# Stick-breaking attention on one Trainium2 core: the sum over later keys carried as one row instead of as a tile

## The reference

```python
z = jnp.einsum('bthd,bshd->bhts', q, k) * (SB_HEAD_DIM ** -0.5)
mask = k_pos[None, :] < q_pos[:, None]
log_fail = jnp.where(mask, jax.nn.log_sigmoid(-z), 0.0)
after = lax.cumsum(log_fail, axis=3, reverse=True) - log_fail
a = jnp.where(mask, jnp.exp(jax.nn.log_sigmoid(z) + after), 0.0)
return jnp.einsum('bhts,bshd->bthd', a, v)
```

## Time and profile before

| what | value |
|---|---|
| median of 3 runs | 1157.36 us |
| the profiled execution | 1159.81 us |
| its span, first to last instruction | 1158.0 us |
| TensorE busy | 1109.8 us, 96% |
| VectorE busy | 739.9 us, 64% |
| ScalarE busy | 466.6 us, 40% |
| GpSimd busy | 278.6 us, 24% |
| chain that ended last | TensorE 88%, VectorE 6%, ScalarE 2% |

### The profile page before, as it was taken

One profiled execution on the slowest core, in us unless ns is written; L12 is line 12 of the kernel. 1 busy time (PEld: TensorE's weight loads), 2 busy tenths in 40 slices (PEclk: granted clock), 3 DMA queues, 4 the chain that ended last, 5 costly groups with the idle time before them and its releaser, 6 DMA issues.

```text
span 1158.0 us, 17212 instructions
## 1 busy us (share of the span) xinstructions
PE 1109.8 (96%) x6486; PEld 1039.7 (90%) x6486; DVE 739.9 (64%) x1347; ACT 466.6 (40%) x923; POOL 278.6 (24%) x306
## 2 busy tenths in 40 slices
PE   3999999999999999999999999999999999999994
PEld 2899988999988999988999987999999999999993
DVE  7747986787986787986787995764332312352228
ACT  4345544155544155543146545346022232242221
POOL 2113422213422213422114422110211100121225
PEclk9999999999999999999999999999999999999997
DMA  6023021115021115021115021205111111111144
GB/s 241 19 71 117 19 91 55 39 46 164 19 92 55 40 39 171 20 91 55 39 40 171 19 91 55 101 19 179 56 37 37 54 39 37 43 49 37 38 182 163
DMA packets 41458, 84.89 MB, mean 73 GB/s; under 512 B 2080, under 2 KB 22176, under 8 KB 41248
## 3 DMA queue, kind: packets, MB, share of 16 engines
q1 hardware_dynamic: 40800, 81.43, 21.6%
q10 hardware_dynamic: 576, 2.36, 0.6%
HBM read 67.27 MB, written 16.52 MB: 72 GB/s over the span
## 4 chain that ended last, share of the span: by engine, by line
PE 88%; DVE 6%; ACT 2%; DMA 1%; issue 1%; SPq 0%; DVEq 0%; ACTq 0%
PE bank L623 56%; PE bank L909 9%; PE bank L699 5%; PE bank L739 5%; PE bank L832 2%; PE bank L855 2%; PE bank L686 2%; PE bank L685 2%; DVE xw L1344 1%; DVE imaskL L1303 1%; DVE yb L1614 1%; PE bank L873 1%; PE bank L783 1%; PE bank L761 1%; DVE St L1530 1%
## 5 line engine op out<-in xcount | busy, mean ns | idle before, releaser
L623 PE MATMUL bank<-xl,wh 128*128 128x384 f32 x1344 | 459.0, 342 | 6.7 <-DVE xl L1340 6.7
L623 PE MATMUL bank<-xh,wh 128*128 128x384 f32 x1344 | 454.9, 338 | 4.3 <-ACT xh L1090 3.5
L623 PE MATMUL bank<-xh,wl 128*128 128x384 f32 x1344 | 456.7, 340 | 0.0
L623 PEld LDWEIGHTS bank<-xl,wh 128*128 128x128 f32 x1344 | 253.5, 189 | 14.3 <-DVE xl L1340 8.1
L623 PEld LDWEIGHTS bank<-xh,wh 128*128 128x128 f32 x1344 | 253.8, 189 | 13.5 <-issue 10.6
L623 PEld LDWEIGHTS bank<-xh,wl 128*128 128x128 f32 x1344 | 253.9, 189 | 7.9 <-issue 4.2
L1244 DVE CAST wh<-wr 128x1024 fp32r<-128x1024 f32 x64 | 51.1, 798 | 102.3 <-PE bank L623 102.3
L1034 ACT ACTIVATE slot<-bank,ngate 128x384 f32<-128x384 f32 x48 | 27.7, 578 | 190.7 <-PE bank L623 188.0
L1701 POOL TENSOR_TENSOR imaskH<-i_nat,k 128x512 fp32r<-128x512 f32 (+1 forms) x36 | 50.5, 1407 | 188.1 <-PE bank L832 188.1
L1246 DVE TENSOR_TENSOR wl<-wr,wh 128x1024 fp32r<-128x1024 f32 x64 | 93.1, 1454 | 2.2
L1713 POOL TENSOR_TENSOR slot<-slot,slot 128x384 f32<-128x384 f32 x24 | 32.7, 1364 | 241.0 <-DVE slot L1579 240.8
(11 more groups left out here) (193 smaller groups left out, 1749.1 us busy)
## 6 DMA issues: line engine op xcount, KB each, us to landing
wr<-wch SPq DMA_DIRECT2D x64, 512.0 KB, 3.7
KTc<-ckT SPq DMA_DIRECT2D x4, 2048.0 KB, 8.9
Vc<-cv SPq DMA_DIRECT2D x4, 2048.0 KB, 8.3
xw<-xT SPq DMA_DIRECT2D x6, 768.0 KB, 10.1
graw<-gated SPq DMA_DIRECT2D x8, 576.0 KB, 5.8
xres<-xT SPq DMA_DIRECT2D x1, 4608.0 KB, 16.6
yT<-yb SPq DMA_DIRECT2D x6, 576.0 KB, 3.0
okT<-kT ACTq DMA_DIRECT2D x4, 576.0 KB, 3.0
```

Source lines behind the costliest of these rows:

```text
L623: i = nc.tensor.matmul(CH[n % 2][:, 0:WIN], weights[:, k, :], rows[:, k, w * WIN:(w + 1) * WIN], start=(m == 0), stop=(m == 23))
```

## The change

The sum over later keys is the same for every key of a tile, and it is already in the bank of the tile before: the log-weight of that tile's first key is its score less the softplus of all its keys and of all later ones. So the kernel after keeps one row. ScalarE copies row 0 of the raw scores to `zr[n % 3]` between Exp and Ln. When the subtraction and the last Exp of that step are done, `later_row` on VectorE subtracts the copy from row 0 of the bank and splits the difference into row 0 (high) and row 32 (low) of `RT[h]`, whose other rows are zero. TensorE adds both with one matmul by `rows_r`, a matrix with ones in rows 0 and 32. `SUM`, `SUH` and `SUL` and all their instructions are gone. Since the bank is now read by `later_row`, the scores of step n also wait for its first instruction for step n - 3. Apart from this the last third of the finish moves from GpSimd to VectorE.

```diff
@@ tensor
                         need(pe, s_a, t - 2)
+                        if n >= 3:
+                            need(pe, s_S, SUMS * p + sums_until(n - 3))
-                        c0 = min(c0, QW // 2)
+                        c0 = row_col(n)
...
                         else:
                             pe.wait_ge(s_sph, SPLITS * p + rows_until(m))
                             add(negtri_r[:, :], SPH[m % 2], c0)
-                            cs = first_col(m - 2)
-                            if q == 1:
-                                pe.wait_ge(s_S, SUMS * p + sums_until(m - 2))
-                                add(negones, SUM[h], cs)
-                            else:
-                                pe.wait_ge(s_Sh, SUM_SPLITS * p + sum_rows_until(m))
-                                add(negones_r[:, :], SUH[h], cs)
-                                pe.wait_ge(s_Sl, SUM_SPLITS * p + sum_rows_until(m))
-                                add(negones_r[:, :], SUL[h], cs)
+                            pe.wait_ge(s_Sl, SUMS * p + sums_until(m - 2))
+                            add(rows_r[:, :], RT[h], row_col(m - 2))
@@ scalar
-                        need(act, s_S, SUMS * p + (sums_until(n - 3) if n >= 3 else 0))
                         nc.scalar.activation(E[n % 3][:, c0:QW], Z[n % 3][:, c0:QW], ACT.Exp).then_inc(s_E, 1)
+                        if STEPS[n][1] > 0:
+                            need(act, s_Sl, SUMS * p + (sums_until(n - 3) if n >= 3 else 0))
+                            nc.scalar.activation(zr[n % 3][0:1, row_col(n):QW], Z[n % 3][0:1, row_col(n):QW], ACT.Copy)
@@ vector
+            def later_row(p, m):
+                h, cols = STEPS[m][2], slice(row_col(m), QW)
+                row = zr[m % 3][0:1, cols]
+                dve.wait_ge(s_a, NS * p + m + 1)
+                V.tensor_tensor(row, Z[m % 3][0:1, cols], row, ALU.subtract).then_inc(s_S, 1)
+                dve.wait_ge(s_S, SUMS * p + sums_until(m))
+                dve.wait_ge(s_rz, 2 * (p + 1))
+                V.tensor_copy(RT[h][0:1, cols], row).then_inc(s_Sh, 1)
+                dve.wait_ge(s_Sh, SUMS * p + sums_until(m))
+                V.tensor_tensor(RT[h][32:33, cols], row, RT[h][0:1, cols].bitcast(F32), ALU.subtract).then_inc(s_Sl, 1)
...
-                        if q > 1:
-                            cs = first_col(n - 2)
-                            dve.wait_ge(s_S, SUMS * p + sums_until(n - 2))
-                            V.tensor_copy(SUH[h][:, cs:QW], SUM[h][:, cs:QW]).then_inc(s_Sh, 1)
-                            dve.wait_ge(s_Sh, SUM_SPLITS * p + sum_rows_until(n))
-                            V.tensor_tensor(SUL[h][:, cs:QW], SUM[h][:, cs:QW], SUH[h][:, cs:QW].bitcast(F32),
-                                            ALU.subtract).then_inc(s_Sl, 1)
+                    if 2 <= n <= NS + 1 and STEPS[n - 2][1] > 0:
+                        later_row(p, n - 2)
...
-                for lo, hi in ((0, 3), (3, 6)):
+                for i, (lo, hi) in enumerate(Y_ROWS):
@@ gpsimd
-                    if 1 <= n <= NS and tile_rank(n - 1) == 1:
-                        later_sum(n - 1)
-                    if n < NS and STEPS[n][1] > 0 and tile_rank(n) != 1:
-                        later_sum(n)
...
-            def finish(w):
-                y, x = yb[:, 6:8, w * WIN:(w + 1) * WIN], xres[:, 6:8, w * WIN:(w + 1) * WIN]
...
```

More of the change, by code:

```diff
@@ L180, in rows_until, with row_col @@
     return sum(tile_rank(i) > 0 for i in range(n + 1))
-def sum_rows_until(n):
-    return sum(tile_rank(i) > 1 for i in range(n + 1))
-SPLITS, SUM_SPLITS = rows_until(NS - 1), sum_rows_until(NS - 1)
+SPLITS = rows_until(NS - 1)
+def row_col(n):
+    return min(first_col(n), QW // 2)
 SW = PAST + P
@@ L271, in build @@
         negtri_r, _ = take("negtri_r", [P, P], F32R)
-        negones_r, _ = take("negones_r", [P, P], F32R)
+        rows_r, _ = take("rows_r", [P, P], F32R)
         bm, _ = take("bm", [P, NBLK + STREAMS])
@@ L281, in build @@
         SPL = [take(f"SPL{i}", [P, QW], F32R)[0] for i in range(2)]
-        SUM = [take(f"SUM{h}", [P, QW])[0] for h in range(2)]
-        SUH = [take(f"SUH{h}", [P, QW], F32R)[0] for h in range(2)]
-        SUL = [take(f"SUL{h}", [P, QW], F32R)[0] for h in range(2)]
+        RT = [take(f"RT{h}", [P, QW], F32R)[0] for h in range(2)]
+        zr = [take(f"zr{i}", [P, QW])[0] for i in range(3)]
+        off[0] += 4 * QW
         aw_o = off[0]
@@ L382, in build @@
         s_sp = sem("softplus")
-        s_S = sem("later_sum")
+        s_S = sem("later_row")
+        s_rz = sem("later_rows_zeroed")
         s_sph = sem("softplus_high")
         s_spl = sem("softplus_low")
-        s_Sh = sem("later_sum_high")
-        s_Sl = sem("later_sum_low")
+        s_Sh = sem("later_row_high")
+        s_Sl = sem("later_row_low")
         s_cr = sem("masks_rounded")
@@ L491, in attention_over @@
             need(eng, s_a, NS * (p + 1))
-            need(eng, s_S, SUMS * (p + 1))
+            need(eng, s_Sl, SUMS * (p + 1))
         def recurrence_over(eng, p, norm=True):
@@ L586, in _ @@
             for w in range(NW):
-                for lo, hi in ((0, 3), (3, 6), (6, 8)):
-                    if lo < 6:
-                        sp.wait_ge(s_yo, 2 * w + lo // 3 + 1)
-                    else:
-                        sp.wait_ge(s_yo3, w + 1)
+                for i, (lo, hi) in enumerate(Y_ROWS):
+                    sp.wait_ge(s_yo, 3 * w + i + 1)
                     r = slice(lo, hi)
@@ L1332, in _ @@
             V.tensor_copy(negtri_r[:, :], negtri).then_inc(s_cr, 1)
-            V.tensor_copy(negones_r[:, :], negones).then_inc(s_cr, 1)
+            V.memset(rows_r[:, :].bitcast(F32), 0.0).then_inc(s_cr, 1)
+            dve.wait_ge(s_cr, 2)
+            for r in (0, 32):
+                i = V.memset(rows_r[r:r + 1, :].bitcast(F32), 1.0)
+            i.then_inc(s_cr, 1)
             dve.wait_ge(s_mt, 1)
@@ L1362, in _ @@
                 recurrence_over(dve, p - 1, norm=False)
+                for h in range(2):
+                    V.memset(RT[h][:, :].bitcast(F32), 0.0).then_inc(s_rz, 1)
                 late = []
@@ L1608, in _ @@
             for w in range(NW):
-                y, x = yb[:, 0:6, w * WIN:(w + 1) * WIN], xres[:, 0:6, w * WIN:(w + 1) * WIN]
+                y, x = yb[:, :, w * WIN:(w + 1) * WIN], xres[:, :, w * WIN:(w + 1) * WIN]
                 dve.wait_ge(s_yr, w + 1)
                 dve.wait_ge(s_ev, OUT_W0 + 20 + 2 * w)
-                for lo, hi in ((0, 3), (3, 6)):
+                for i, (lo, hi) in enumerate(Y_ROWS):
                     V.tensor_tensor(y[:, lo:hi, :], y[:, lo:hi, :], yrs[w][:, None, :].broadcast_to([P, hi - lo, WIN]),
                                     ALU.mult).then_inc(s_yg, 1)
-                    dve.wait_ge(s_yg, 2 * w + (1 if lo == 0 else 2))
+                    dve.wait_ge(s_yg, 3 * w + i + 1)
                     if w == 0:
@@ L1650, in _ @@
             for p in range(PAIRS):
-                def later_sum(n):
-                    h, q = STEPS[n][2], tile_rank(n)
-                    c0, t = first_col(n), NS * p + n
-                    src, dst = E[n % 3], SUM[h]
-                    pool.wait_ge(s_sp, t + 1)
-                    if q == 0:
-                        need(pool, s_Sl, SUM_SPLITS * p + sum_rows_until(n))
-                        G.tensor_copy(dst[:, c0:QW], src[:, c0:QW]).then_inc(s_S, 1)
-                        return
-                    if q == 1:
-                        pool.wait_ge(s_cum, t + 1)
-                    else:
-                        pool.wait_ge(s_Sl, SUM_SPLITS * p + sum_rows_until(n))
-                    pool.wait_ge(s_S, SUMS * p + sums_until(n - 2))
-                    lo = first_col(n - 2)
-                    if lo > c0:
-                        G.tensor_copy(dst[:, c0:lo], src[:, c0:lo])
-                    G.tensor_tensor(dst[:, lo:QW], dst[:, lo:QW], src[:, lo:QW], ALU.add).then_inc(s_S, 1)
                 recurrence_over(pool, p - 1, norm=False)
@@ L1730, in _ @@
                     add_square(k, w)
-            pool.wait_ge(s_xr, 16)
-            add_square(KT_N - 2, 0)
-            add_square(KT_N - 2, 1)
-            finish(0)
-            add_square(KT_N - 2, 2)
-            finish(1)
-            finish(2)
+            for w in range(NW):
+                add_square(KT_N - 2, w)
 def constants():
```

13 lines of the change are left out of this document (3 added, 10 removed).

## The result

The kernel after takes 1245.82 us, the median of 4 runs (1245.64 to 1248.04), beside 1157.51 us for the kernel before in the same comparison (1157.12 to 1159.33). The ratio is 1.0764, with a 95% interval of 1.0745 to 1.0783: slower, as forecast, by 7 us more than the 1239 I had given, and inside the range.

A forecast was written before the change was run, and what follows sets the result against it. The prediction took TensorE's own instructions to bound the attention stage. Four pairs of 19.8 + 2.2 - 1.1 us, less 2.3 for the finish, gave +81.3: 1241 us profiled, 1239 median, 8-in-10 range 1190 to 1262.

The forecast's parts named there:

- The new wait: Attention stage: scores of each step wait for a chain begun at the previous step's scores, some 19 times a pair.
- The chain's length: Scores to next scores: 4.95 us for full tiles, 5.15 diagonal, 4.28 at 384 columns, 3.4 at 256; +19.8 us a pair.
- Late work of VectorE: Between chains: weight split 0.8 us late, gating 0.55, five copies 0.8; +2.2 us a pair.
- The clock: TensorE's clock in the stage's new gaps: nothing in the main forecast, since shorter waits need not cost anything.
- rival 2: TensorE's clock falls in the gaps of both diagonal blocks, about 1.4 us each: 1250 to 1264 us; chance 0.13.
- One-row instructions: Row copy and subtraction in the chain: a one-partition instruction costs as much as a full one with as many columns.
- Rival 1: One-row instructions in the chain are short, a full chain taking 4.06 us: +42, so 1199 us; chance 0.15.
- What goes: SUL matmuls removed from TensorE, counting only between steps 8 and 10 and after 23: 1.1 us a pair saved.
- GpSimd beside VectorE: Mask in the chain stays at its median as GpSimd's sums go; 27 us for continued hindrance left out.
- The finish: End of kernel: scaling all rows on VectorE alone ends it at 1151.2 instead of 1153.5, saving 2.3 us.
- The sum: Whole kernel: 4 x (19.8 + 2.2 - 1.1) - 2.3 = +81.3 us, profiled execution from 1159.81 to 1241.
- Rival 3: Attention stage: the wait doesn't bind, TensorE stays full, 12.0 us of SUL and 2.3 of finish saved: 1143 us; chance 0.07.

The follow-up runs named there:

- e2: The kernel before, with scores of step n also waiting for VectorE's split of step n - 1, no row instruction added: 1221.77 us, ratio 1.0543.
- e3: The kernel after, with the row subtraction moved ahead of the newest step's split on VectorE: 1197.71 us, ratio 1.0333 to the kernel before.
- e6: The kernel after, with ScalarE copying finished row 0 to SBUF, so scores wait only for the last Exp: 1177.94 us, ratio 1.0156 to the kernel before.
- e7: As e6, with the raw row copied one iteration later, behind the next step's Ln: 1177.1 us, ratio 1.0146 to the kernel before.
- e8: As e7, with the three row instructions on GpSimd instead of VectorE: 1161.81 us, ratio 1.0021 to the kernel before.

## Why the prediction was right

**The new wait.** Right. It was to be some 19 waits a pair; the trace has 16 (64 in four pairs), of 82.4 us in all. e2 shows that the wait alone costs 63 of the 92 us, and e3 that the place of the instruction waited for decides how much. e6 shows the other side of it: with no wait on VectorE for the bank, 70 us are gone (ratio 1.0156 for 1.0764) while every row instruction is still there.

**The chain's length.** Right within 0.21 us a step, and within 0.02 for the even full tiles. Full tiles off the diagonal take 4.97 in the even stretch from step 20 on (4.95 forecast), diagonal ones 5.31 and 5.16 (5.15), tiles of 384 columns 4.28 (4.28), of 256 columns 3.57 and 3.55 (3.4), those behind steps 6 and 7 4.99 and 4.84 (4.78), behind 22 4.79 (4.58), where VectorE's split also waited 0.17 us for TensorE. The row copy adds less than worked out: from Exp to Ln it is now 342.23 - 341.26 = 0.97 in the place of 0.63, so 0.34 and not 0.37. What was short was the last link: from the end of the row subtraction to the scores' start it is 345.68 - 345.54 = 0.14 us, not the 0.05 that I had estimated. In a full tile the limit comes 2.36 us behind the scores for the 2.42 worked out and the subtraction takes 0.67 for 0.69, so that the errors nearly cancel, which is luck. In steps 2 to 8 the link is short in all six intervals, 0.5 us of the 0.6 by which they were missed; at 256 columns I had also dropped the last digit, 0.06 each, the split of step 6 is 0.14 slow (below), and the shorter way to the limit gives some of it back.

**Late work of VectorE.** Right for the gating and the weight split, wrong for the copies. In 10 to 16 it was to add 0.55 and 0.8, and the block is +9.66 for the forecast's +9.65, but by luck. The gating makes the limit of step 11 0.6 late (interval 4.08). The five copies of iteration 12 cost nothing: the intervals 12 to 13 and 13 to 14 are 4.29 as in steps 4 to 6, and VectorE stood idle for 0.27 us before the limit that follows them. What took the place of their 0.8 is interval 10 to 11 with 3.88: the scores of step 10 met no wait, and queued in TensorE behind the values of an earlier step, so that Exp began 0.84 us after their start and not 0.44 to 0.51. The weight split gives 17 to 18 5.83, which is the 4.95 with 0.8 added and 0.08 more. The 0.25 in the interval ahead of it (5.22) was not in the sum; it is a split of VectorE slowed beside GpSimd (below).

**The clock.** This is the term that was too small, since I had it at nothing. After the late weight split TensorE waits, and then runs slowly (timeline of TensorE, kernel after; the matmul by SPH takes 0.39 to 0.40 at the full clock):

```profile
356.73 0.47 PE L686 MATMUL bank<-QS,KS 128*128 128x512 f32 x1 [1.89 <-DVE zr L1299]
...
359.30 0.63 PE L700 MATMUL bank<-SPH,negtri_r 128*128 128x512 f32 x1
```

The slow matmuls come into the chain by the split, whose buffer the subtraction still reads (timeline of VectorE):

```profile
360.88 0.43 DVE L1395 CAST SPH<-E 128x512 fp32r<-128x512 f32 x1 [1.10 <-PE bank L700]
```

The next two intervals are 6.04 and 5.29 in the place of 4.97, 1.4 us a pair or 5.6 in all, in each of the four pairs of this execution. So rival 2 was partly true, at one place a pair instead of one in each diagonal block, and with the price that the earlier trace rows gave. The Trainium skill (TensorE: Matmul & The Clock Gate, Part 1) has TensorE at 1.2 GHz by default and released by activity; what fell here agrees with that, but by it I had argued that shorter waits need not cost anything, and a wait of 1.89 us did.

**One-row instructions.** Taken at the full price, and right: 0.67 and 0.57 us for one row where 128 rows take 0.69 and 0.60. Rival 1 would have needed 0.17.

**What goes.** The saving of 1.1 a pair was 0.61 between steps 8 and 10 and about 1 behind step 23, so slightly low. In e6, e7 and e8 the same matmul is worth 1.2 to 1.6 us in the seven full tiles, once nothing waits for the bank.

**GpSimd beside VectorE.** I left 27 us out on the ground that GpSimd has one product a step left, and the mask shows this was nearly right: a median of 0.300 and 0.440 at most. What is left shows in the split: in all four pairs the second part takes 0.83 us at step 6 and 0.92 to 0.94 at step 16 for the 0.69 of the same shape elsewhere, each time while a GpSimd instruction runs (timeline of VectorE, kernel after). That is 0.4 us a pair.

```profile
349.23 0.93 DVE L1397 TENSOR_TENSOR SPL<-E,SPH 128x512 fp32r<-128x512 f32 x1
```

By the rule of the Trainium skill that I had weighed (SBUF — State Buffer, Who interferes with whom) the mask should get cheaper as the sums go, and it did, by 0.036 at the median.

**The finish.** Right in its cause, short in size: 2.3 forecast, 4.4 measured in the spans. VectorE's end was worked out to half a microsecond; that one store in the place of two would be left behind VectorE's end was not thought of.

**The sum.** Per pair 23.07 for 20.9: 1.4 for the clock, 0.6 in steps 2 to 8, mostly the semaphore, and 0.6 in the other full tiles, less 0.5 more of saving. Times four that is 8.7 us too low, against 2.1 more than forecast from the finish and the 1.7 that is mostly the clock in the kernel before, together 4.9; so the closeness of the total owes something to errors of both signs. The profiled execution after took 1245.98 where 1241 was forecast. The rest of the 7 us is the step from the profiled execution to the median, which I had taken at 2.45 as in the kernel before, and which is 0.16 here.

**Rival 3** falls by the waits of the kernel after, and by e2. Its 12.0 us of matmuls did not show in the time of any kernel, since each way of making the row that was tried brought a wait of its own.

## What to carry to other kernels

A wait costs what stands in the waited-for engine's queue in front of the instruction, so before an instruction takes over the reading of a shared buffer, add up the chain from the producer's own start to that instruction's end and compare it with the distance that the ring of buffers has allowed so far; where it is longer, the ring has lost its depth. Making work smaller by a factor of 128 in rows saved next to nothing on VectorE and ScalarE here (0.67 for 0.69 us, 0.57 for 0.60), and such a row still has to be waited for. Of a change with several parts, measure each alone: here the small part was the gain.
